# Two-layer transformer on one core: where NSA preparation copies, multiplies and scores, and how the last gate and up columns are laid out

## What is computed

```python
def swiglu(x, w_gate, w_up, w_down):          # D 1024, D_FF 2816
    return (silu(x @ w_gate) * (x @ w_up)) @ w_down

def compress(k, pos_emb, w1, b1, w2):         # 15 windows of 32 tokens, stride 16
    blocks = k[:, idx] + pos_emb[:, None, :]
    ...
    return gelu(blocks @ w1 + b1) @ w2        # hidden 128

def nsa_mixer(...):                           # 16 heads, 2 groups, head size 64
    q, kc, vc, ks, vs, kw, vw, gates = split(x @ w_in)
    k_cmp, v_cmp = compress(kc, ...), compress(vc, ...)
    ...
    o = g0 * o_cmp + g1 * o_slc + g2 * o_win
    return o @ w_out
```

## Time and profile before

| what | value |
|---|---|
| median of 3 runs | 1055.97 us (1055.48 to 1056.35) |
| the profiled execution | 1055.41 us, span 1053.6 us |
| mean granted clock | 0.988 |
| PE busy | 1026.6 us, 97% of the span |
| DVE, ACT, POOL busy | 587.2, 475.9, 115.0 us |

### The profile page before, as it was taken

One profiled execution on the slowest core, in us unless ns is written; L12 is line 12 of the kernel. 1 busy time (PEld: TensorE's weight loads), 2 busy tenths in 40 slices (PEclk: granted clock), 3 DMA queues, 4 the chain that ended last, 5 costly groups with the idle time before them and its releaser, 6 DMA issues.

```text
span 1053.6 us, 13214 instructions
## 1 busy us (share of the span) xinstructions
PE 1026.6 (97%) x5260; PEld 863.6 (82%) x5260; DVE 587.2 (56%) x590; ACT 475.9 (45%) x633; POOL 115.0 (11%) x149
## 2 busy tenths in 40 slices
PE   9999999999999999999999999999997899999997
PEld 7888988888898888898888888898876778888885
DVE  6654544755746644462666444544677575455444
ACT  7443533425674445452443334433455445454430
POOL 0010000324900100000012000000024320000000
PEclk9999999999999999999999999999997999999998
DMA  9677453740312755464456644564532155456531
GB/s 343 241 266 242 163 199 128 239 160 1 121 41 85 254 201 178 159 206 153 167 202 240 230 159 159 171 228 152 202 125 81 40 194 205 159 164 215 181 120 40
DMA packets 79934, 179.58 MB, mean 170 GB/s; under 512 B 3248, under 2 KB 13632, under 8 KB 79888
## 3 DMA queue, kind: packets, MB, share of 16 engines
q1 hardware_dynamic: 77408, 170.21, 46.5%
q0 software_dynamic: 2480, 8.72, 2.6%
HBM read 177.87 MB, written 1.05 MB: 170 GB/s over the span
## 4 chain that ended last, share of the span: by engine, by line
PE 91%; DVE 5%; issue 1%; ACT 1%; POOL 1%; DMA 0%; POOLq 0%; DVEq 0%; ACTq 0%
PE acc L1353 26%; PE acc L1351 26%; PE acc L1352 26%; PE trb L1410 5%; PE acc L1579 2%; PE acc L1558 1%; PE acc L1466 1%; PE acc L1463 1%; DVE neg_max L1056 1%; PE acc L1467 1%; DVE norm_gb L1301 1%; PE aux L1620 1%; PE aux L1558 1%; POOL y L565 0%; DVE xt_lo L907 0%
## 5 line engine op out<-in xcount | busy, mean ns | idle before, releaser
L897 DVE TENSOR_TENSOR w_lo<-raw,w_hi 128x2048 fp32r<-128x2048 f32 x148 | 337.7, 2285 | 211.6 <-ACT w_hi L623 211.4
L623 ACT ACTIVATE w_hi<-raw 128x2048 fp32r<-128x2048 f32 x149 | 284.0, 1908 | 200.2 <-PE acc L1353 197.3
L1351 PE MATMUL acc<-w_hi,xt_hi 128*128 128x512 f32 (+1 forms) x960 | 366.8, 382 | 1.2 <-DVE xt_lo L907 1.2
L1353 PE MATMUL acc<-w_hi,xt_lo 128*128 128x512 f32 (+1 forms) x960 | 360.1, 375 | 0.0
L1352 PE MATMUL acc<-w_lo,xt_hi 128*128 128x512 f32 (+1 forms) x960 | 359.6, 375 | 0.0
L1353 PEld LDWEIGHTS acc<-w_hi,xt_lo 128*128 128x128 f32 x960 | 181.2, 189 | 33.1
L1351 PEld LDWEIGHTS acc<-w_hi,xt_hi 128*128 128x128 f32 x960 | 181.5, 189 | 32.1 <-issue 2.3
L1352 PEld LDWEIGHTS acc<-w_lo,xt_hi 128*128 128x128 f32 x960 | 181.7, 189 | 30.2
L1353 PE MATMUL acc<-w_hi,ht_lo 128*128 128x512 f32 x352 | 138.7, 394 | 0.0
L1352 PE MATMUL acc<-w_lo,ht_hi 128*128 128x512 f32 x352 | 138.0, 392 | 0.0
L1351 PE MATMUL acc<-w_hi,ht_hi 128*128 128x512 f32 x352 | 137.4, 390 | 0.0
(11 more groups left out here) (193 smaller groups left out, 829.5 us busy)
## 6 DMA issues: line engine op xcount, KB each, us to landing
raw<-ffn_w_down SPq DMA_DIRECT2D x44, 1024.0 KB, 4.9
raw<-ffn_w_gate SPq DMA_DIRECT2D x42, 1024.0 KB, 5.2
raw<-ffn_w_up SPq DMA_DIRECT2D x42, 1024.0 KB, 5.6
raw<-w_kv SPq DMA_DIRECT2D x8, 1024.0 KB, 5.3
raw<-w_in SPq DMA_DIRECT2D x6, 1024.0 KB, 5.5
raw<-w_out_a SPq DMA_DIRECT2D x4, 1024.0 KB, 5.7
raw<-w_q SPq DMA_DIRECT2D x4, 1024.0 KB, 5.5
raw<-w_out_b SPq DMA_DIRECT2D x4, 1024.0 KB, 5.6
```

The costliest lines, as they stand in the source:

```text
L623: act.activation(w_hi[:, slot, 0:k * c], raw[:, slot, 0:k * c], ACT.Copy).then_inc(hi_ready, 1)
L897: dve.tensor_tensor(w_lo[:, slot, 0:k * c], raw[:, slot, 0:k * c], w_hi[:, slot, 0:k * c].bitcast(F32), ALU.subtract).then_inc(lo_ready, 1)
L1351: pe.matmul(out_ap, s_hi, hi, start=first, stop=False)
L1353: return pe.matmul(out_ap, s_lo, hi, start=False, stop=last)
```

## The change

Four edits.

1. ACT instead of POOL doubles the compression's keys and values: two instructions of 128x256 for each token tile (the source read twice through a broadcast). Tile 0's stand between the splits of units 5 and 6 of `nsa_in`, tile 1's after unit 7. POOL goes straight to the rotations. On DVE the splits of the rotated keys (`split_beside`) move from before both window blocks to between them.
2. `hidden` is cut into pieces. `hidden(0)`: four pieces of 4 products, each ahead of one row tile of the last unit of token tile 0. `hidden(1)`: eight pieces of 2 products, ahead of the row tiles of units 0 and 1 of token tile 1. `second_layer` moves from ahead of unit 2 to ahead of unit 3.
3. In NSA attention, where a step's value job opens a turn, the scores of job i+1 are issued ahead of `nsa_first`, and not again in the next step. Turn 0's `nsa_first` moves from value job 0 to value job 1. (The diff has `j == 1` in place of `j == 0`.)
4. Gate and up are handed over as one matrix: gate's first 2560 columns, up's first 2560, gate's last 256, up's last 256. The last group's two units are now row halves of the last 512 columns, multiplied by `columns_unit`: 48 products of 512 columns instead of 96 of 256. Silu reads the first half of one bank, `gated` the second.

```diff
@@ scalar
+            def duplicate(tok):
+                act.wait_ge(acc_free, FILL_OF["nsa_in", 0, tok] + 1)
+                for j, c in enumerate((KC, VC)):
+                    src = kv_a[:, tok, c:c + 2 * DH].rearrange("p (g d) -> p g d", d=DH).unsqueeze(2)
+                    ins = act.activation(y[:, tok, j * 256:(j + 1) * 256].rearrange("p (g r d) -> p g r d", g=2, r=2),
+                                         bc(src, P, 2, 2, DH), ACT.Copy)
+                ins.then_inc(k_dup, 1)
-            split_units(n0 + 4, n0 + 8)
+            split_units(n0 + 4, n0 + 6)
+            duplicate(0)
+            split_units(n0 + 6, n0 + 8)
+            duplicate(1)
@@ vector
-            for k in range(2):
-                split_beside(k)
             for b in range(2):
+                if b:
+                    for k in range(2):
+                        split_beside(k)
...
+                    up = acc[:, 2 * tok + 1] if c == 512 else acc[:, 2 * tok, HALF:2 * HALF]
@@ tensor, hidden and the order of nsa_in
-                for pair in range(CMP_BLOCK // 2):
+                for pair in range(k * pairs // of, (k + 1) * pairs // of):
...
-            group(0, e + 2, n0 + 4, range(4), columns_unit, {2: lambda: turn_kc(0), 3: lambda: turn_kc(1)})
+            group(0, e + 2, n0 + 4, range(4), columns_unit, {2: lambda: turn_kc(0), 3: lambda: turn_kc(1)},
+                  inner={3: {k: lambda k=k: hidden(0, k, 4) for k in range(4)}})
             group(1, e + 3, n0 + 4, range(4), columns_unit,
...
+                  inner={j: {k: lambda j=j, k=k: hidden(1, 4 * j + k, 8) for k in range(4)} for j in range(2)})
@@ tensor, attention
-                if j == 0 or jobs[j - 1][3]:
+                if j == 1 or ends_turn_at(jobs, j - 1):
                     first(turn_no)
...
-                if sc:
...
+                if sc and not ends_turn_at(NSA_JOBS, pv - 2):
+                    nsa_scores(i)
...
+                if ends_turn_at(NSA_JOBS, pv - 1) and i + 1 < len(NSA_JOBS):
+                    nsa_scores(i + 1)
                 if pv >= 0:
                     values("nsa", NSA_JOBS, pv,
@@ tensor and SP, FFN tail
-                group(0, e0 + 2 * g + 2, n0 + 4 * g + 4, range(2), half_unit,
+                group(0, e0 + 2 * g + 2, n0 + 4 * g + 4, range(2), columns_unit,
...
-                load(n0 + 4 * G_FULL, rows(wg, 0, KT, 512 * G_FULL, HALF))
-                load(n0 + 4 * G_FULL + 1, rows(wu, 0, KT, 512 * G_FULL, HALF))
+                for half in range(2):
+                    load(n0 + 4 * G_FULL + half, rows(w_gate_up[i], half * 512, 4, 2 * full, 512))
```

More of the change, by code:

```diff
@@ L108, in ends_turn, with ends_turn_at @@
     return j >= 0 and jobs[j][3] and jobs[j][0] == turn
+def ends_turn_at(jobs, j):
+    return j >= 0 and jobs[j][3]
 def jobs_through(jobs, turn):
@@ L1366, in columns_unit @@
                 return ins
-            def half_unit(n, j, tok):
-                hi, lo = weights(w_hi, n), weights(w_lo, n)
-                for kt in range(KT):
-                    ins = three(acc[:, 2 * tok + j, 0:HALF], xt_hi[:, kt, tok * P:(tok + 1) * P],
-                                xt_lo[:, kt, tok * P:(tok + 1) * P], hi[:, kt, :], lo[:, kt, :], kt == 0,
-                                kt == KT - 1)
-                return ins
             def rows_unit(s_hi, s_lo, tiles):
@@ L1613, in swap_halves, with hidden @@
                 pe.matmul(trb[:, t % 2], swap, src, start=True, stop=True).then_inc(tr_full, 1)
-            def hidden(b):
-                copied("kc", b)
-                pe.wait_ge(w1_in, 32)
+            def hidden(b, k, of):
+                if k == 0:
+                    copied("kc", b)
+                    pe.wait_ge(w1_in, 32)
                 w = w1k if b == 0 else w1v[:]
-                for pair in range(CMP_BLOCK // 2):
+                pairs = CMP_BLOCK // 2
+                for pair in range(k * pairs // of, (k + 1) * pairs // of):
                     ins = pe.matmul(aux[:, b, 0:2 * N_CMP], w[:, pair, :], blk[:, b, pair, :], start=(pair == 0),
-                                    stop=(pair == CMP_BLOCK // 2 - 1))
-                ins.then_inc(hid_full, 1)
+                                    stop=(pair == pairs - 1))
+                if k == of - 1:
+                    ins.then_inc(hid_full, 1)
             def second_layer():
@@ L1656, in _ @@
             group(1, e + 1, n0, range(4), columns_unit, None, ("x", "ffn0", 1))
[L1657 removed]
+            group(0, e + 2, n0 + 4, range(4), columns_unit, {2: lambda: turn_kc(0), 3: lambda: turn_kc(1)},
+                  inner={3: {k: lambda k=k: hidden(0, k, 4) for k in range(4)}})
             group(1, e + 3, n0 + 4, range(4), columns_unit,
[L1659 to L1662 removed]
+                  {1: lambda: turn_q(0), 2: lambda: (turn_kr(0), turn_kr(1)),
+                   3: lambda: (second_layer(), *(swap_halves(("ks", m), ("kr", m),
+                                                             nks[:, 0, m].rearrange("p g t -> p (g t)"))
+                                                 for m in range(2)))},
+                  inner={j: {k: lambda j=j, k=k: hidden(1, 4 * j + k, 8) for k in range(4)} for j in range(2)})
             compressed_scores(0)
@@ L1679, in _, with nsa_scores @@
             pe.wait_ge(acc_free, e + 3)
-            for i, sc, tr, pv in job_steps(NSA_JOBS):
+            def nsa_scores(i):
                 if i < 8 and i % 2 == 0:
@@ L1684, in _ @@
                     copied("qr", "nsa", 1, i // 4 - 2)
+                if i >= 3:
+                    pe.wait_ge(exp_done, i - 2)
+                scores(NSA_JOBS, i, score_bank[i % 3], lambda h, m: nqs[:, h], lambda h, m, part: nks[:, part, m, h // 8])
+            for i, sc, tr, pv in job_steps(NSA_JOBS):
                 if i == 0:
@@ L1855, in ffn, with gate_up @@
         return [dram(f"ffn{b}_{which}_{layer}", a[f"ffn{b}_{which}"][layer]) for layer in range(DEPTH) for b in (1, 2)]
+    def gate_up():
+        full = 512 * G_FULL
+        return [dram(f"ffn{b}_gate_up_{layer}", np.concatenate(
+            [a[f"ffn{b}_w_{which}"][layer][:, cols] for cols in (slice(0, full), slice(full, FF))
+             for which in ("gate", "up")], axis=1)) for layer in range(DEPTH) for b in (1, 2)]
     def two(name):
@@ L1864 @@
         dram("squares", constants()[1]),
[L1865 removed]
+        gate_up(), ffn("w_down"),
         dram("norm_gain", a["ln_g"].reshape(3 * DEPTH, D)),
```

26 lines of the change are left out of this document (7 added, 19 removed).

## The result

The changed kernel takes 1047.11 us in the median (1046.64 to 1049.92); the kernel before took 1055.89 beside it. The ratio is 0.9944, 95% interval [0.9919, 0.9969], which carries 1055.97 to 1050.1 us, against a forecast of 1047.2 and a range up to 1049.8. The quotient of the two medians alone is 0.9917, 8.8 us, which looks like the forecast come true; with four executions on each side that is luck. Executions of either kernel differ by up to 9.7 us with the clock that they are granted, so a comparison needs many of them. Over all executions the mean spans are 1046.1 us for the changed kernel (26 executions, these four among them, mean clock 0.9895) and 1052.8 us for the one before (103 executions beside the experiments, 0.9887): the change gives 6.7 us, +- 1.0. The sum of the prediction was 8.6. Five further executions, with spans of 1604 to 4645 us, are left out.

A forecast was written before the change was run, and what follows sets the result against it. PE's stream of wide products was taken to bound the kernel. Terms 2.5 + 1.9 + 1.6 + 2.6 = 8.6 us off 1055.4 gave 1046.8, or 1047.4 against the median; forecast 1047.2 us, range 1045.0 to 1049.8.

The forecast's parts named there:

- The sum: Whole kernel: 2.5 + 1.9 + 1.6 + 2.6 = 8.6 us gained, from columns, doubled keys, clock and scores.
- What bounds: PE's stream of wide products; gains only from removing products, filling holes in PE's stream or raising its clock.
- Last columns: Last gate and up columns of four FFNs: 512-column products replace pairs of 256, gaining 2.5 us.
- Doubled keys: Ahead of the `turn_kc` transposes: doubling on ACT removes PE's whole hole, gaining 1.9 us.
- the slack of 0.5 us at the key blocks: DVE's key blocks end at 220.2, PE reaches the first piece of `hidden(0)` at 220.75; tightest place of this part.
- The clock, 1.6: Wide products behind `hidden(0)`: cutting the narrow products into pieces removes the half-clock stretch, gaining 1.6 us.
- a changed pattern of clocks in differential attention: Differential attention's windows: a pattern of clocks other than before would show the prediction wrong.
- The two rivals of chance 0.12 each: Clock falls anyway in the mixed stretch, 1048.8; or falls depend on the moment, 1045.6 or 1048.8. Chance 0.12 each.
- The cutting: Compression's products in pieces among wide ones: no gain or loss taken, bounds 1.1 us either way.
- Scores at turn changes: NSA attention, holes ahead of `nsa_first`: filled by the next job's scores, 2.6 us gained, bounds 1.3 to 2.9.
- 310.4: Out projection behind NSA attention: predicted to start near 310.4 instead of 316.6, a sign in the trace.
- ACT and DVE take the gain back: NSA attention's chains of jobs 7, 11 and 19: gain 1.3 instead of 2.6 us, 1048.5; chance 0.10.

The follow-up runs named there:

- e2: Changed kernel with the last gate and up columns back at 96 products of 256 columns in each FFN; median 1049.39 us.
- e5: Changed kernel with only the doubling of the compression's keys and values back on POOL (GpSimd); ratio to the kernel before 0.9949.
- e17: Changed kernel with 4 and 3 unread wide products ahead of two waiting transpose groups in differential attention; median 1045.59 us.
- e6: Changed kernel with the preparation as before: doubling on POOL and the compression's products in two blocks; median 1049.92 us.
- e4: Changed kernel with only the compression's products back in two blocks, ahead of units 0 and 1 of the last group; median 1048.49 us.
- e10: Changed kernel with every compression product issued twice, still in pieces among wide products (16 and 8 for 4 and 2 pairs' worth omitted); median 1069.45 us.
- e11: Changed kernel with the selected scores back in their own step and turn 0's first product at value job 0, second timing; median 1050.79 us.
- e12: The changed kernel without any edit, timed again; median 1048.39 us, ratio to the kernel before 0.9939.

## Why the prediction missed, step by step

**What bounds.** Right: removing products, filling holes and raising the clock are the three things that paid, in e2, e5 and e17.

**Last columns: 2.5 predicted, 2.0 to 2.1 measured.** The mechanism holds. The distances are 0.227 as predicted in the steady part, yet each FFN gave 0.50 to 0.57 and not 0.63. Behind the transposes the mean distances are 0.2273 for 512 columns ((458.56 - 453.56) / 22) and, in e2, 0.1198 for 256 ((461.68 - 456.17) / 46), a gain of 0.0123 a pair, 0.59 a FFN; the rest stays open.

**Doubled keys: 1.9, right.** The hole went whole and comes back with POOL; the slack of 0.5 us at the key blocks was 0.7 in fact.

**The clock, 1.6: the step that failed.** It took a fall seen in one execution as a certain cost of the block, caused by its length and the hole before it. The profile of e6 has block and hole and no fall; that of e4 has the block and no fall; the changed kernel has neither and falls at 255 us in all four of its profiles. Over all executions the mean clock rose by 0.0008, that is 0.0008 x 1050 x 0.85 = 0.7 us, with an interval of +- 0.8, and no part of this can be laid to the cut. The prediction had named a changed pattern of clocks in differential attention as a sign of being wrong, and it came. The two rivals of chance 0.12 each were both half right: the clock falls all the same, though behind the mixed stretch and not in it, and when it does differs between executions. The prediction's evidence against them, a clock of 1.00 at 780 to 785 and behind `hidden(1)`, was one draw of something that varies. A profile shows one draw; a term that rests on the clock wants the spread of the runs beside it.

**The cutting: nothing predicted, -0.2 measured** (27.59 against 27.40 us), well inside its bounds.

**Scores at turn changes: 2.6 predicted, 1.4 measured**, at the low bound of 1.3 and for a reason I had not named. The out projection starts at 311.56, not at 310.4. I looked for what is late next on DVE and ACT, and took the waits for DVE as DVE's own lateness. Part of it was DVE's wait for POOL, and when PE came earlier the multiplication that waits grew from 0.52 to 0.99 us. The rival "ACT and DVE take the gain back" gave nearly the right size (1.3) with the wrong cause: DVE was early enough, and POOL's subtraction held it. I had weighed the shared interfaces for the key rotations, where they cost nothing, and not where POOL runs 16 subtractions beside DVE's mix.

**The sum.** 2.1 + 1.9 - 0.2 + 1.4 = 5.2 us at full clock, with 0.7 for the clock 5.9, against 6.7 +- 1.0 measured. In the fit the part at equal clock is 6.0 +- 0.5 and so 0.8 above the terms, or 5.8 +- 0.6 and 0.6 above with a constant for each chip; what that is stays open. The sum was 1.9 too high: 1.2 of the scores, 0.9 of the clock (1.6 against 0.7), 0.4 of the columns and 0.2 of the cutting, less the 0.8 not accounted for. So part of its closeness is luck: the terms alone missed by 2.7.

## What to carry to other kernels

Where the granted clock falls in a stage with holes, try a few wide products in them: four profiles had 6.8 to 10.2 us at half clock in place of 13.6 to 17.1, and the stage took 1.7 us less. Compare kernels on the same chip, or by the starts in their traces: one kernel's mean span differed by 3.9 us between chips. Do not expect narrow products to be cured by spreading them among wide ones; if there are enough to lower the clock, a block confines the slow time and pieces stretch it. When an engine's small operation has a length that changes with its start, look for an operation on another engine that ends with it, before taking that length into a chain.

## What the chip showed beyond that

- One program's executions ranged from 1048.1 to 1057.8 us of span (the kernel before) with mean clocks of 0.984 to 0.994.
- PE 100% busy is no safeguard: e10 stood at half clock for 41 us without an idle moment in its windows.
- A fall can be free: 4 us at clock 0.57 (255 to 259) cost 0.14 us of the stage (67.16 against 67.02), and the waits of 0.56 and 0.36 us at the turn changes, which e17 has, are gone there. In e11, with the scores in their turn, a fall of the same length cost 2.4 (70.82 against 68.44), and 7 us at 0.51 in e12 cost 3.2.
- A DVE multiplication of 128x16 took 0.17 to 1.02 us, by where POOL's subtraction stood.
- POOL's 128x32 multiplications took 2.2 us beside DVE's splits, and 0.25 without them.
